# Modulation units given out in twos instead of ones between halves of products

## The reference, cut to what matters

```python
ada = jax.nn.silu(c) @ w_ada[l] + b_ada[l]              # (1, 2048) @ (2048, 12288)
sh1, sc1, gt1, sh2, sc2, gt2 = jnp.split(ada, 6, axis=-1)
h = modulate(rmsnorm(x, norm1_g[l]), sh1, sc1)
proj = h @ w_in[l]                                       # q, k, v, indexer, pooled part
...
x = x + gt1 * (jnp.concatenate([attn_out, pool_out], -1) @ w_out[l])
h2 = modulate(rmsnorm(x, norm2_g[l]), sh2, sc2)
x = x + gt2 * hier_moe(h2, ...)                          # 32 experts, top 2 within one group
```

## Time and profile before

| | us |
|---|---|
| three runs | 2449.99, 2454.22, 2456.52 |
| median | 2454.22 |
| the profiled execution: its own time | 2448.66 |
| its span, first to last instruction | 2446.8 |
| PE busy | 2104.9 (86%) |
| DVE busy | 1214.5 (50%) |
| ACT busy | 898.2 (37%) |

### The profile page before, as it was taken

The page is one execution under the profiler, slowest core; times in us unless marked ns, Lnnn a source line. Parts: engine busy times, 40 slices in busy tenths (PEclk is TensorE's granted clock), DMA queues, the critical chain, the costliest instruction groups (busy, mean ns, idle before and its releaser), DMA issues.

```text
span 2446.8 us, 38264 instructions
## 1 busy us (share of the span) xinstructions
PE 2104.9 (86%) x14524; PEld 1399.7 (57%) x14524; DVE 1214.5 (50%) x2205; ACT 898.2 (37%) x1382; POOL 0.2 (0%) x4
## 2 busy tenths in 40 slices
PE   5699998986887888887878887899989799998987
PEld 1377776862222222222222222799889799997887
DVE  1544785454333333333333334647875554477555
ACT  1333434441112111221112221546865444466543
POOL 0000000000000000000000000000000000000000
PEclk9899999998999999999999999899999899998999
DMA  9988775966999999999999997364445455543442
GB/s 378 404 310 300 255 279 194 340 245 273 422 422 421 422 422 422 422 422 422 422 422 422 422 422 299 113 199 146 137 140 179 129 172 182 181 139 107 134 128 97
DMA packets 135046, 695.44 MB, mean 284 GB/s; under 512 B 14992, under 2 KB 15120, under 8 KB 85264
## 3 DMA queue, kind: packets, MB, share of 16 engines
q1 hardware_dynamic: 134928, 693.81, 74.2%
HBM read 691.66 MB, written 2.10 MB: 284 GB/s over the span
## 4 chain that ended last, share of the span: by engine, by line
PE 50%; DMA 37%; DVE 7%; ACT 4%; issue 2%; SPq 1%; DVEq 0%; ACTq 0%
PE acc L1000 34%; DMA ring<-in_w 33%; DMA land<-in_stream_a 4%; PE acc L997 3%; PE psS L1226 3%; PE psO L1050 3%; DVE WL L1662 1%; ACT WH L1378 1%; SPq L880 1%; PE psM L1081 1%; ACT SB L1448 1%; DVE HL L1672 0%; PE psT L946 0%; PE psM L1214 0%; PE psM L1050 0%
## 5 line engine op out<-in xcount | busy, mean ns | idle before, releaser
L1000 PE MATMUL acc<-HH,WH 128*128 128x256 f32 x2552 | 749.0, 293 | 40.7 <-DVE HL L1684 15.4
L1000 PE MATMUL acc<-HH,WL 128*128 128x256 f32 x2552 | 727.9, 285 | 0.0
L1000 PE MATMUL acc<-HL,WH 128*128 128x256 f32 x2552 | 727.4, 285 | 0.0
L1662 DVE TENSOR_TENSOR WL<-land,WH 128x1024 fp32r<-128x1024 f32 (+1 forms) x350 | 425.6, 1216 | 420.6 <-ACT WH L1378 416.5
L1000 PEld LDWEIGHTS acc<-HH,WH 128*128 128x128 f32 x2552 | 495.3, 194 | 81.7 <-issue 14.5
L1000 PEld LDWEIGHTS acc<-HH,WL 128*128 128x128 f32 x2552 | 495.9, 194 | 3.3 <-issue 2.2
L1000 PEld LDWEIGHTS acc<-HL,WH 128*128 128x128 f32 x2552 | 495.4, 194 | 0.0
L1378 ACT ACTIVATE WH<-land 128x1024 fp32r<-128x1024 f32 (+1 forms) x350 | 368.0, 1051 | 248.6 <-PE acc L1000 198.9
L1226 PE MATMUL psS<-ring,low 128*32 128x512 f32 x2048 | 282.3, 664 | 148.9 <-DMA ring<-in_w 126.7
L1226 PEld LDWEIGHTS psS<-ring,low 128*32 128x32 f32 x2048 | 53.4, 113 | 339.3 <-DMA ring<-in_w 253.0
L2046 DVE TENSOR_REDUCE SB<-psT 128x128 f32<-128x512 f32 x32 | 22.1, 692 | 389.0 <-PE psT L1236 389.0
(11 more groups left out here) (326 smaller groups left out, 1989.0 us busy)
## 6 DMA issues: line engine op xcount, KB each, us to landing
ring<-in_w SPq DMA_DIRECT2D x384, 1024.0 KB, 24.1
land<-in_stream_a SPq DMA_DIRECT2D x284, 512.0 KB, 7.5
land<-in_stream_bc SPq DMA_DIRECT2D x246, 512.0 KB, 3.8
land<-in_stream_bc SPq DMA_DIRECT2D x12, 384.0 KB, 3.2
X<-in_xT SPq DMA_DIRECT2D x1, 2048.0 KB, 15.8
out<-low SPq DMA_DIRECT2D x4, 512.0 KB, 2.7
cst<-in_const SPq DMA_DIRECT2D x1, 1538.0 KB, 12.3
low<-in_w_pool SPq DMA_DIRECT2D x1, 1024.0 KB, 4.9
```

Of the source, the lines that this page charges most:

```text
L1000: mm = pe.matmul(bank[:, 0:S], w[:, kk, :], h[:, rows[kk], :], start=(z == 0 and i == 0), stop=stop)
L1662: ins = dve.tensor_tensor(WL[:, q % PARTS, 0:n], land[k][:, p % LAND[k], 0:n], WH[:, q % PARTS, 0:n].bitcast(F32), ALU.subtract)
```

## The change

`between()` waits until two units are owed and then gives out two, one behind the other.

```diff
@@ order_a(), between()
-        while owed[0] >= 1 and left:
-            owed[0] -= 1
-            b, q = left.pop(0)
-            ada(b, q)
+        while owed[0] >= 2 and left:
+            for _ in range(2):
+                owed[0] -= 1
+                b, q = left.pop(0)
+                ada(b, q)
```

## The result

| | before | the change |
|---|---|---|
| median, 20 runs each | 2451.82 us | 2458.72 us |
| lowest and highest | 2448.53, 2459.58 | 2452.83, 2464.09 |
| the profiled execution, and its span | 2448.66, 2446.8 | 2457.2, 2455.4 |

The ratio of the runs is 1.0022 with a 95% interval of 1.0012 to 1.0031: slower by 3 to 8 us. Its middle, 5.4 us, is inside the 0.3% that the text counts as no change. The profiled execution is 8.5 us slower than the one of before, where the sum said 0.7; only one of the twenty runs of before was faster than 2448.66, so part of the 8.5 may be that. So the forecast of "no change" and its range held, and the working behind it did not: two terms were wrong (the saving from `p2` to `p7` and the waits for weight loads), and the experiments say how.

What follows compares the result with a forecast made beforehand. PE was taken to bound most stretches, with the expert loop shifted whole; -0.7 - 1.3 + 2.0 - 1.9 + 2.6 = +0.7 us on 2448.66, plus 5.6 for the median, gave 2455 us, range 2447 to 2463.

Steps and rivals of the forecast that it cites:

- Stretch k0 to (q, 7), -0.7: From k0 to (q, 7): 32 units in 16 gaps instead of 32 make the stretch 0.7 us shorter.
- Behind (q, 7), -1.3: Behind (q, 7): four units leave, `topk 0` starts earlier, giving back only 1.3 us; PE idles 6.6 us.
- The clock fall, +2.0: Behind the new idle time before `rot (q, 6)`: PE's granted clock falls, costing 2.0 us.
- p2 to p7, -1.9: From p2 to p7: 12 units in 6 gaps instead of 10 save 1.9 us, one unit hidden beside DVE.
- wo, +2.6: In `wo`: 20 units instead of 16, mostly in pairs, cost 2.6 us more on an always busy PE.
- Weight loads, 0: In `wo`: bunched pieces could make PE wait nothing to 2 us; taken as 0.
- The sum, +0.7: Whole kernel: all terms together make the profiled execution 0.7 us slower, 2449.4 us.
- rival 1: At some nine pairs: bunched loads stall PE 1.63 us each, +14.7 us, time 2470; chance 0.07.
- Rival 2: Idle time is shorter or costs no clock, and the fall at 415 us vanishes: -3.8 us, 2451; chance 0.11.
- rival 3: Half clock lasts up to `(p, 3)` and falls once more behind it: 2 x 2.5 us on top, 2460; chance 0.08.

Runs made afterwards that it cites:

- e9: The change, with 45 useless matmuls ahead of `rot (q, 6)`, placed before its wait; ratio to the kernel before 1.0021.
- e12: The change, with 45 useless matmuls ahead of `rot (q, 6)` and 16 more ahead of the pooled matmuls and around the first half of `(wo, 0)`; ratio 1.0026.
- e1: The kernel before, units still in ones, but only 32 of them up to `(q, 7)`, leaving 20 for `wo`; ratio 1.0019.
- e10: The kernel before, with 20 useless matmuls in four places where PE waits; ratio 0.9966.
- e2: The change, units in twos, with four more units given out behind `(q, 7)`, so the stretches have the counts of before; ratio 1.0036.
- e11: The kernel before, ones, 32 units up to `(q, 7)`, four beside `topk 0`, useless matmuls as in e10 but 18 ahead of `rot (q, 6)`; ratio 0.9970.
- e5: The change, with 45 useless matmuls ahead of `rot (q, 6)`, placed behind its wait for DVE; ratio 1.0028.

## Why the prediction was right, and where not

- **Stretch k0 to (q, 7), -0.7.** It ended 0.3 us earlier (`(q, 7)` done at 299.49 in place of 299.80), with 2.5 us of waits for pieces up to there in place of 1.8. Right within its bounds. That a fall of the clock went at 230 us and another came at 153 was not in the working.
- **Behind (q, 7), -1.3.** `topk 0` started 1.56 us earlier, the idle time was 6.95 us where 6.6 was worked out, `rot (q, 6)` came 1.55 us earlier. Right. That 7 us of PE time taken out here would give only this back was the best step of the working.
- **The clock fall, +2.0.** It came, and cost about 2.4 us at its place (`e9`) and 2.5 at `S 3` (`e12`; `e1` says the same in ones, 62.3 us from `rot (q, 6)` to `S 3` where before has 59.8). Mechanism and size were right up to there. But taken away it gave nothing at the end of `wo`, because in twos the pieces were then waited for. The term should have been asked the same question as the units: what is late next when it goes.
- **p2 to p7, -1.9.** Together with the fall the forecast was +0.1 from `rot (q, 6)` to `S 3`; it was +3.2 (63.0 us in place of 59.8). With the fall taken away it was +0.7 (60.5, `e12`), so this term failed by 2.6 us and the fall makes up the other 2.5. The step that failed is "The second unit of that pair is hidden beside DVE's 9 us", with the 1.4 us of saving ahead of it. The unit's piece lands late, PE waits 1.64 us for it in `e12` (1.25 in the change), and from `rot (q, 6)` to `topk 1` it takes 29.4 us where before has 28.8 and 27.4 was forecast. Behind `topk 1` the wait for DVE's sum of a block comes back (1.61 us; 1.62 in the change, before has 1.71 ahead of `topk 1`), and the 0.5 us of saving that was forecast there does not show: 31.1 us up to `S 3`, 31.0 before.
- **wo, +2.6.** It was +6.1 (127.6 us from `(wo, 0)` to the loads, 121.4 before). The count is right: `e1`, with its 20 units in ones, has +3.9. By the prices that is 4 x 1.18 + 0.5 = 5.2, less the 1.1 us by which its fall at 417 is cheaper (47 matmuls in 7.20 us and 38 before, 9 x 0.124). The pairs should save 2.6 of the 5.2; with the waits of 4.1 and the cheaper fall (49 matmuls, 1.4) that makes 2.6 + 4.1 - 1.4 = 5.3, and 0.8 us stays unassigned.
- **Weight loads, 0.** This is the term that was mis-sized, at "waits of nothing to 2 us are possible, and I take 0". PE's waits for pieces came to 4.7 us more than before (8.3 less 3.6), 4.1 of them in `wo`. The reason given for 0, that four slots are free at once and the queue is short, does not fit what the chain shows: SP asks for the pieces in a row only when a late `WL` lets it go on, and they land after 7 to 9 us. The 6.5 us to a landing, worked out beside it, was near (5.95 and 7.9 us at the two places shown); the maximum of 9.1 in the row should have decided, not the median.
- **The sum, +0.7,** was +8.5 in the profiled execution and +5.4 (3 to 8) in the runs. Of rival 1 (pairs stall, 1.63 us at nine of them) the mechanism was there, in nine waits of 0.9 us on average. Rival 2 (the fall at 415 goes) happened by half, 1.4 us. That the time lies in the range is in part luck: the range reached to rival 3 and over the spread of the runs, and what filled it was not what it was made for.

## What to carry to other kernels

When a change takes PE work out of one place and rounding puts it into another, cost the places apart: a unit is free beside DVE's `topk` and costs 1.18 us in a stretch bound by PE. Here the move of four of them, with the fall of the clock in the place that they left, was three quarters of the loss in the trace. Of a gain or a loss ahead of a serial chain (remainder, slot, issue, landing) nothing need arrive behind it, so a term counts only if the next thing that is late is later by it: 4.2 us gained ahead of `wo` in `e12` moved the loads by none. And a version in which one fall of the clock is taken away has to be looked through for another, before it is read as "worth nothing" (`e9` against `e12`). Bunching what a queue has to fetch is paid by the queue's depth, before its rate: here one landing slot less cost twos 14 us of waits and ones 8.

## What the runs showed of the hardware

- Idle times of 2.65 and 2.9 us on PE had the granted clock fall to 1.2 GHz behind them, for up to 6.2 us; filled with 16 useless matmuls, which leave at most 0.7 us of idle time in a piece, the clock stayed at 2.4 GHz (`e10`). Of this case's versions it is the only kind that made the kernel faster.
- The length of one idle time did not decide by itself whether the clock fell: it fell behind 2.03 us (`e2`, 306.21), 1.97 (`e11`, 348.81) and 2.36 (`e9`, 340.37), and it did not behind 3.13 us ahead of `(wo, 0)` in the kernel before (1.00 from 400 to 410 us), where `e9` has 0.83 behind the same 3.13.
- A matmul of 256 columns took 0.124 us at full clock (5.56 us for 45 in `e9`), and 0.168 on average where the clock had fallen before it and came back on the way (7.57 for 45 in `e5`).
- A piece of 512 KB landed after 6.9 us at the median from 110 to 300 us in the change (6.2 before) and after 7.4 from 425 to 515 us; the one shown above took 9.23.
